# A conditioned decoder block on one core: no spare matmuls between the constants and the first projection

## The chip, the core and the metric

The kernel runs on one NeuronCore of one Trainium2 chip. The metric is the device time of one execution, in microseconds (us); lower is better. Three timed executions of the kernel before are shown, and one execution taken by the hardware profiler.

## What is computed

The reference is one decoder layer over 512 tokens of 1024 features, all in float32. What matters here is how it begins: a vector `c` gives the shifts and scales (`mod`), `x` is normalised and modulated, and the result `h` is multiplied by a wide weight matrix.

```python
c_act = jax.nn.silu(c)
mod = c_act @ w_ada[l] + b_ada[l]                      # (1, 6 * 1024)
shift1, scale1, gate1, shift2, scale2, gate2 = jnp.split(mod, N_MOD, axis=-1)
h = modulate(rmsnorm(x, g_norm1[l]), shift1, scale1)   # (512, 1024)
z = h @ w_in[l]
xr, gr, q, k, v, fl, mg = jnp.split(z, split_idx, axis=-1)
# RG-LRU over xr, forgetting attention over q, k, v, merged by gates,
# then a gated ffn and a last modulated rmsnorm
```

## The kernel before, in words

Each engine has an order of its own, written out by hand, and the engines meet at semaphores. The features lie on the 128 partitions and the 512 tokens along the free dimension. Every float32 matrix is split into a high and a low part of type `fp32r`, and a product is three matmuls (`mm3`, lines 1667 to 1669): low times high, high times low, high times high.

The start is what the change touches, and the orders there are these.

- GpSimd writes the constants: `ident` (the unit matrix), `ones`, `ones_r` and others. TensorE waits for them (`consts`, 8).
- SyncE issues nearly all loads, in this order: `c`, `x` in four blocks, seven small vectors, four blocks of `w_ada` of 1 MB each (`ada_first` 0 to 3), three halves of weight tiles of `w_in`, `ada_first` 4 to 7, and the other halves of these tiles. `ada_first` 6 goes into the buffer of block 0, so it waits until TensorE is done with the first column sum (`ada_mm`, 1).
- ScalarE squares and normalises `x` (lines 612 and 621), copies the transposed blocks out of PSUM (line 626), takes the high parts of the weight tiles (line 637), and when `mod` is there it makes `htmp` and the high part of `h`, feature block by feature block (`h_high`, lines 642 and 645).
- VectorE sums part of the rows of `w_ada` times `c` (lines 1006 and 1009), stores the first scales and shifts (`ada_first_store`, lines 1016, 1019 and 1023), and makes the low parts: `lo_half` for weights (line 1152), `h_low` for `h` (line 1157). Between the two halves of `h` it works on 25 small steps for the recurrence (`lam_first`, `lam_rest`).
- TensorE transposes small vectors (lines 1732, 1759 and 1760), multiplies some rows of `w_ada` with `c` one column at a time (`ada_piece`, line 1711), transposes the four blocks of `x` (`x_transposes`, line 1743), adds what VectorE has summed (`ada_first_total`, line 1719), and then begins the first projection in `project2` (lines 1789 on).

Between these stand calls of `keep_clock(n)`: n float32 matmuls of `ones` with `ident` into PSUM bank 1, which nobody reads. There are four such calls, of 8, 25, 3 and 8 matmuls. The trace has two records for one float32 matmul, so 8 matmuls are 16 records; a transpose is one record.

After the start the projections, the recurrence, the attention, the output projection and the ffn follow, with two weight tiles in a ring. Each load of the ring waits until VectorE is done with the tile before it, so these loads have no time of their own but follow the engines.

Of the kernel before, what the change touches and what calls it, by code (L numbers as in the profile page):

```python
# [81 lines left out]
def hybrid_block(nc, x, c, w_ada, b_ada, g_norm1, w_in, w_rnn_conv, b_rnn_conv, w_lru_a, b_lru_a,  # L82
# [4 lines left out]
    with ctx:  # L87
# [1576 lines left out]
        def _(te):  # L1664
# [38 lines left out]
            def ada_piece(g, v, k, begin=False):  # L1703

                q = 4 * g + 2 * v + k // 4
                te.wait_ge(ada_first_loaded[q], 16)
                if g:
                    te.wait_ge(ada_out, v + 1)
                for j in range(4):
                    at_ = 4 * g + j  # L1710
                    te.matmul(ps[:, 7 - v, at_:at_ + 1], ada_first[:, q % 6, k % 4, P * j:P * j + P], cact[:, k:k + 1],  # L1711
                              start=begin and j == 0, stop=False, skip_group_check=True)

            def ada_first_total(g, v):

                te.wait_ge(ada_part, ada_summed(g, v) + len(ADA_DVE[g, v]))
                for j in range(4):
                    at_ = 4 * g + j
                    ins = te.matmul(ps[:, 7 - v, at_:at_ + 1], (ada_acc, ada_acc2)[v][:, P * j:P * j + P], ones[:, 0:1],  # L1719
                                    start=False, stop=True, skip_group_check=True)  # L1720
                ins.then_inc(ada_mm, 1)

            def keep_clock(n, bank=0):

                for _ in range(n):
                    te.matmul(ps[:, bank, 0:P], ones[:, :], ident[:, :], start=True, stop=True)  # L1726
# [4 lines left out]
            te.wait_ge(vec_a_loaded, 16 * 3)  # L1731
            te.transpose(ps[:, 0, 0:V_ROWS_A], vrows[0:V_ROWS_A, 0], ident[0:V_ROWS_A, 0:V_ROWS_A])\
              .then_inc(vec_mm, 1)
            keep_clock(25, 1)

            def x_transposes(b):
                te.wait_ge(xn1_done, b + 1)
                if b >= 2:
                    te.wait_ge(xT_copied, 2 * b - 2)
                for half in range(2):  # L1740
                    for j in range(4):
                        k = 4 * half + j
                        ins = te.transpose(ps[:, 2 + 2 * (b % 2) + half, P * j:P * j + P],
                                           x_nat[:, b, P * k:P * k + P], ident[:, :])
                    ins.then_inc(xT_mm, 1)
# [2 lines left out]
            x_transposes(0)  # L1748
            x_transposes(1)
            ada_piece(0, 0, 4)  # L1750
            keep_clock(3, 1)
            x_transposes(2)
            ada_piece(0, 1, 0, begin=True)
            x_transposes(3)
# [6 lines left out]
            ada_piece(0, 1, 4)  # L1761
            ada_piece(0, 1, 5)
            ada_first_total(0, 1)
            keep_clock(8, 1)
            te.wait_ge(vec_ok, 2)
            te.wait_ge(xT_copied, 2 * NB)

# [362 lines left out]
```

## Time and profile before

| | us |
|---|---|
| median of three timed executions | 983.5 |
| lowest, highest | 982.2, 983.51 |
| the profiled execution | 983.65 |
| its span, first to last instruction | 981.9 |
| TensorE matmuls busy in it | 968.5 (99%) |
| VectorE, ScalarE busy | 635.5 (65%), 415.8 (42%) |
| mean granted TensorE clock | 0.993 of full |

The page cuts the span into 40 slices of 24.5 us. Each digit is a busy share in tenths, and PEclk is the granted clock in tenths of full speed:

```profile
PE   8999999999999999999999999999999999999997
DVE  3789998522668797853758555777674344754665
ACT  6479777322426354352623373322232222422331
PEclk9899999999999999999999999999999999999999
DMA  9743311334674435432217505666532332233201
```

TensorE is busy nearly all the time. The change lies in the first two slices.

### The profile page before, as it was taken

To read this page: it belongs to the slowest core of one execution; us is meant where nothing else is said; L and a number is where in the kernel's file an instruction comes from. 1 tells how busy PE (TensorE), PEld (TensorE's weight loads), DVE (VectorE), ACT (ScalarE), POOL (GpSimd) and SP (SyncE) were. 2 spreads that over 40 slices of the span, in tenths; PEclk is the share of its full clock that TensorE was granted. 3 is DMA by queue.
4 is the path that set the end of the run, shared out by engine and by line. 5 is a ranking of instruction groups with operands and counts; after the bars stand their busy time and mean duration, and the time that the engine had idled before them with its cause. 6 is when DMAs were issued, how large, how long until landed. Compare 5 with 4: busy or idle time off the path is not lost.

```text
span 981.9 us, 12554 instructions
## 1 busy us (share of the span) xinstructions
PE 968.5 (99%) x4739; PEld 816.5 (83%) x4739; DVE 635.5 (65%) x856; ACT 415.8 (42%) x548; POOL 2.2 (0%) x12
## 2 busy tenths in 40 slices
PE   8999999999999999999999999999999999999997
PEld 8878887788888888989888889888888888888875
DVE  3789998522668797853758555777674344754665
ACT  6479777322426354352623373322232222422331
POOL 0000000000000000000000000000000000000000
PEclk9899999999999999999999999999999999999999
DMA  9743311334674435432217505666532332233201
GB/s 326 249 139 102 102 43 49 96 96 131 210 232 151 153 116 181 129 107 86 86 44 259 192 21 172 196 200 202 180 118 86 105 109 85 86 106 136 100 20 67
DMA packets 105775, 129.37 MB, mean 132 GB/s; under 512 B 4636, under 2 KB 81156, under 8 KB 105612
## 3 DMA queue, kind: packets, MB, share of 16 engines
q1 hardware_dynamic: 105192, 126.75, 39.5%
q10 hardware_dynamic: 548, 2.14, 0.6%
q8 instruction: 23, 0.38, 0.2%
q14 instruction: 12, 0.10, 0.0%
HBM read 126.77 MB, written 2.11 MB: 131 GB/s over the span
## 4 chain that ended last, share of the span: by engine, by line
PE 94%; DVE 3%; DMA 1%; SPq 1%; issue 0%; ACT 0%; DVEq 0%; ACTq 0%
PE ps L1667 30%; PE ps L1669 30%; PE ps L1668 30%; DMA ada_first<-in_w_ada 1%; PE ps L1900 1%; PE ps L1711 1%; DVE wsplit_x L1570 0%; DVE wraw_x L1566 0%; PE ps L1726 0%; PE ps L1719 0%; PE ps L1701 0%; PE ps L1700 0%; PE ps L2017 0%; DVE act_s L1583 0%; SPq L447 0%
## 5 line engine op out<-in xcount | busy, mean ns | idle before, releaser
L1667 PE MATMUL ps<-h,wsplit 128*128 128x512 f32 (+1 forms) x816 | 312.7, 383 | 1.2 <-DVE h L1539 1.2
L1669 PE MATMUL ps<-h,wsplit 128*128 128x512 f32 (+1 forms) x816 | 310.9, 381 | 0.0
L1668 PE MATMUL ps<-h,wsplit 128*128 128x512 f32 (+1 forms) x816 | 310.8, 381 | 0.0
L988 DVE TENSOR_TENSOR wsplit<-wraw,wsplit 128x2048 fp32r<-128x2048 f32 (+2 forms) x79 | 167.0, 2114 | 101.6 <-ACT wsplit L596 64.1
L1667 PEld LDWEIGHTS ps<-h,wsplit 128*128 128x128 f32 x816 | 153.6, 188 | 29.9 <-issue 1.4
L1669 PEld LDWEIGHTS ps<-h,wsplit 128*128 128x128 f32 x816 | 153.4, 188 | 29.5
L1668 PEld LDWEIGHTS ps<-h,wsplit 128*128 128x128 f32 x816 | 153.5, 188 | 28.8
L596 ACT ACTIVATE wsplit<-wraw 128x2048 fp32r<-128x2048 f32 (+2 forms) x69 | 120.9, 1752 | 105.2 <-PE ps L1669 104.8
L1596 DVE SCALAR_TENSOR_TENSOR cv<-ps,vec,cv 128x511 f32<-128x511 f32 (+1 forms) x48 | 35.9, 748 | 55.7 <-ACT cv L945 52.6
L1041 DVE SCALAR_TENSOR_TENSOR ada_acc<-ada_raw,small,ada_acc 128x512 f32<-128x512 f32 x84 | 63.1, 751 | 2.7
L1667 PE MATMUL ps<-wsplit,act_s 128*128 128x512 f32 x160 | 62.3, 390 | 0.7 <-DVE act_s L1583 0.7
L1669 PE MATMUL ps<-wsplit,act_s 128*128 128x512 f32 x160 | 62.3, 389 | 0.0
L1668 PE MATMUL ps<-wsplit,act_s 128*128 128x512 f32 x160 | 62.2, 389 | 0.0
L945 ACT ACTIVATE cv<-ps,vec 128x512 f32<-128x512 f32 x24 | 18.7, 778 | 101.1 <-PE ps L1669 101.1
L1669 PE MATMUL ps<-wsplit,h 128*128 128x256 f32 (+1 forms) x160 | 48.7, 304 | 0.0
L1668 PE MATMUL ps<-wsplit,h 128*128 128x256 f32 (+1 forms) x160 | 48.7, 304 | 0.0
L1667 PE MATMUL ps<-wsplit,h 128*128 128x256 f32 (+1 forms) x160 | 48.7, 304 | 0.0
L929 ACT ACTIVATE wsplit<-wraw 128x2048 fp32r<-128x2048 f32 x10 | 19.2, 1916 | 61.6 <-PE ps L1669 52.4
L1606 DVE TENSOR_TENSOR act<-gg,ps 128x512 f32 (+1 forms) x24 | 16.4, 685 | 34.7 <-PE ps L1669 34.7
L785 ACT ACTIVATE qk<-ps 128x512 fp32r<-128x512 f32 x16 | 9.6, 598 | 63.2 <-PE ps L1669 63.2
L1667 PEld LDWEIGHTS ps<-wsplit,act_s 128*128 128x128 f32 x160 | 30.0, 188 | 7.2 <-issue 1.1
L1669 PEld LDWEIGHTS ps<-wsplit,act_s 128*128 128x128 f32 x160 | 30.0, 188 | 6.3
(248 smaller groups left out, 1415.7 us busy)
## 6 DMA issues: line engine op xcount, KB each, us to landing
wraw<-in_w_ffn_up SPq DMA_DIRECT2D x24, 1024.0 KB, 5.1
wraw<-in_w_in SPq DMA_DIRECT2D x23, 1024.0 KB, 5.3
ada_raw<-in_w_ada SPq DMA_DIRECT2D x16, 1024.0 KB, 6.7
wraw<-in_w_ffn_down SPq DMA_DIRECT2D x10, 1024.0 KB, 4.9
ada_first<-in_w_ada SPq DMA_DIRECT2D x8, 1024.0 KB, 12.1
ada_raw<-in_w_ada_final SPq DMA_DIRECT2D x8, 1024.0 KB, 5.1
wraw<-in_w_in SPq DMA_DIRECT2D x12, 512.0 KB, 3.8
wraw<-in_w_proj_rnn SPq DMA_DIRECT2D x8, 640.0 KB, 4.4
```

Source lines behind the costliest of these rows:

```text
L596: ae.activation(wsplit[:, s, HI, 0:n], wraw[:, s, 0:n], ACT.Copy).then_inc(w_hi, 1)
L929: ae.activation(wsplit[:, s, HI], wraw[:, s], ACT.Copy).then_inc(w_hi, 1)
L945: ae.activation(cv[:, t], ps[:, t, :], ACT.Identity, scale=vec[:, ds(V_FW + 2 * NF + t + 2 * i, 1)], bias=vec[:, ds(V_FB + t + 2 * i, 1)]) ...
L988: ve.tensor_tensor(wsplit[:, s, LO, 0:n], wraw[:, s, 0:n], wsplit[:, s, HI, 0:n].bitcast(F), ALU.subtract).then_inc(w_lo, 1)
L1041: ve.scalar_tensor_tensor(acc[:, :], w, cact[:, k:k + 1], acc[:, :], ALU.mult, ALU.add)\
L1596: ve.scalar_tensor_tensor(cv[:, t, d:T], ps[:, t, 0:T - d], vec[:, ds(V_FW + (2 - d) * NF + t + 2 * i, 1)], cv[:, t, d:T], ALU.mult, ALU.a ...
L1606: ve.tensor_tensor(act[:, 2 * i + t], gg[:, t], ps[:, 2 + t, :], ALU.mult)\
L1667: te.matmul(dst, lhs(LO), rhs(HI), start=start, stop=False)
L1668: te.matmul(dst, lhs(HI), rhs(LO), start=False, stop=False)
L1669: return te.matmul(dst, lhs(HI), rhs(HI), start=False, stop=stop)
L1711: te.matmul(ps[:, 7 - v, at_:at_ + 1], ada_first[:, q % 6, k % 4, P * j:P * j + P], cact[:, k:k + 1], start=begin and j == 0, stop=False, ...
L1900: ins = te.transpose(ps[:, bank, at_:at_ + P], prob[:, t, pcol:pcol + P], ident[:, :])
```

## The change

Three of the four calls of `keep_clock` go: that of 25 matmuls behind the transpose of the first small vectors, that of 3 between the transposes of `x`, and that of 8 ahead of the first projection. The call of 8 right after the constants (line 1730) stays. Nothing else is changed, moved or added.

```diff
             te.transpose(ps[:, 0, 0:V_ROWS_A], vrows[0:V_ROWS_A, 0], ident[0:V_ROWS_A, 0:V_ROWS_A])\
               .then_inc(vec_mm, 1)
-            keep_clock(25, 1)
...
             x_transposes(0)
             x_transposes(1)
             ada_piece(0, 0, 4)
-            keep_clock(3, 1)
             x_transposes(2)
...
             ada_piece(0, 1, 4)
             ada_piece(0, 1, 5)
             ada_first_total(0, 1)
-            keep_clock(8, 1)
             te.wait_ge(vec_ok, 2)
             te.wait_ge(xT_copied, 2 * NB)
```

## Rows read from the trace of the kernel before

**Rows 1.** The page, part 4: who carries the chain that ended last.
```profile
PE 94%; DVE 3%; DMA 1%; SPq 1%; issue 0%; ACT 0%; DVEq 0%; ACTq 0%
```

**Rows 2.** The chain of waits, first 45 us: start us, us, what.
```profile
7.83 14.47 DMA ada_first<-in_w_ada
...
22.34 3.45 PE ps L1711 x16
25.79 1.71 PE ps L1719 x8
27.50 3.62 PE ps L1726 x16
31.12 0.43 PE ps L1667
...
33.32 0.23 PE ps L1667
```

**Rows 3.** Timeline of TensorE: start, us, line, out<-in, xcount [idle before <-releaser].
```profile
3.10 3.78 PE L1726 MATMUL ps<-ident,ones 128*128 128x128 f32 x16 [3.10 <-POOL ones_r L585]
6.68 0.35 PE L1732 MATMUL ps<-ident,vrows 88*128 88x88 f32 x1
6.83 6.75 PE L1726 MATMUL ps<-ident,ones 128*128 128x128 f32 x50
13.42 0.95 PE L1711 MATMUL ps<-small,ada_first 128*128 128x1 f32 x8
14.23 1.95 PE L1743 MATMUL ps<-ident,x_nat 128*128 128x128 f32 x16
...
16.82 0.91 PE L1726 MATMUL ps<-ident,ones 128*128 128x128 f32 x6
...
21.53 0.30 PE L1760 MATMUL ps<-ident,vrows 96*128 96x96 f32 x1
22.34 3.45 PE L1711 MATMUL ps<-small,ada_first 128*128 128x1 f32 x16 [0.51 <-DMA ada_first<-in_w_ada]
...
53.08 0.47 PE L1667 MATMUL ps<-h,wsplit_r 128*128 128x512 f32 x1 [1.05 <-DVE h L1157]
```

**Rows 4.** TensorE by half microseconds: stretch, length, busy (records), clock, DMA share, GB/s.
```profile
8.00:8.50 0.50, 0.50 (x4) 1.00 0.94 359
...
9.00:9.50 0.50, 0.50 (x7) 1.00 0.79 223
...
22.00:22.50 0.50, 0.16 (x2) 1.00 1.10 346
22.50:23.00 0.50, 0.50 (x4) 0.51 1.11 354
...
32.50:33.00 0.50, 0.50 (x3) 0.75 1.06 389
```

**Rows 5.** Timeline of VectorE in the first 62 us.
```profile
13.26 0.48 DVE L1006 TENSOR_SCALAR ada_acc<-ada_first,small 128x512 f32<-128x512 f32 x1 [0.97 <-DMA ada_first<-in_w_ada]
...
29.35 0.69 DVE L1157 TENSOR_TENSOR h<-htmp,h 128x512 fp32r<-128x512 f32 x1 [0.28 <-ACT h L645]
...
48.56 0.17 DVE L1127 TENSOR_SCALAR small<-small 128x10 f32<-128x10 f32 x1
49.25 0.16 DVE L1023 TENSOR_TENSOR mod<-ps,vec 128x4 f32<-128x4 f32 x1 [0.52 <-PE ps L1719]
...
52.24 1.29 DVE L1157 TENSOR_TENSOR h<-htmp,h 128x512 fp32r<-128x512 f32 x2
```

**Rows 6.** Timeline of ScalarE in the first 62 us.
```profile
20.22 1.08 ACT L626 ACTIVATE xT_out<-ps 128x512 f32<-128x512 f32 x2 [0.71 <-PE ps L1743]
...
27.84 0.81 ACT L642 ACTIVATE htmp<-xT_out,mod,small 128x512 f32<-128x512 f32 x1 [1.46 <-DVEq L1027]
```

**Rows 7.** Timeline of SyncE's DMA issues in the first 75 us.
```profile
17.79 8.24 SPq L433 DMA_DIRECT2D ada_first<-in_w_ada  x4
```

**Rows 8.** DMA issues of the same stretch: count, KB each, median us to landing.
```profile
ada_first<-in_w_ada SPq DMA_DIRECT2D x8, 1024.0 KB, 12.1
```

## The prediction

> **What bounds the kernel now.** I read the page's chain first: TensorE carries 94% of it [rows 1], so the kernel is a long row of matmuls, and a microsecond lost by TensorE at the start is lost at the end unless a later wait gives it back. Then the chain of the first 45 us, since the change ends before 31 us: the load of `w_ada` block 3 ends at 22.30, TensorE works from 22.34 to 27.50 on single-column matmuls (24 records), then 3.62 us on the last spare matmuls, and the first projection starts at 31.12 [rows 2]. Third TensorE's own timeline, to see the spare work (16, 50, 6 and 16 records) beside the real work [rows 3], and last the clock by half microseconds. The reader is to see two things there. The clock column says 1.00 at 8 us and at 9 us, but 4 records fit into a half microsecond at the one and 7 at the other [rows 4]: before about 8.9 us the engine ran at its lower level, 1.2 GHz, whatever the column shows before its first change. It then ran at 2.4 GHz until 22.5, fell to 0.50, and rose at 32.75 (0.75 as the mean of 32.5 to 33.0) [rows 4].
>
> What TensorE did before each change: 5.8 us of full-width matmuls without a break (3.10 to 8.9) before the first rise, 5.25 us of the same (27.50 to 32.75) before the second. The fall came in the idle 0.51 us behind single-column matmuls and small transposes, when the last spare matmul was nearly 5 us past [rows 2 to 4].
>
> **The change part by part.** It removes 36 matmuls, 72 records.
>
> The 25: TensorE has nothing to do from about 7.0 us (end of the small transpose) until `ada_first` 0 lands, which is by VectorE's row just before 13.26 [rows 3, 5]. The first `ada_piece` starts at 13.42 now, so the matmuls themselves hold it up by 0.15 us: that is the whole direct gain, -0.15. In their place stand 6.2 us of idling. No row of before has so long an idle time of TensorE after a rise; the nearest is the 0.51 us before 22.34, at whose end the clock was at half. So I take the clock as down at 13.26. (Before, at 13.3, it was up.)
>
> From there the same work at the lower level. Up to the small vectors it is 64 records: three `ada_piece` of 8, 32 transposes, `ada_first_total` of 8. At half clock a record of the single-column kind takes 5.16 us / 24 = 0.215 us [rows 2]; a full-width record takes 3.62 / 16 = 0.226 [rows 2] against 0.91 / 6 = 0.15 with its tail or 1.95 / 16 = 0.12 for the transposes at full clock [rows 3]. The trace has no transpose of `x` at half clock: the bounds are 0.12 (not slower) and 0.233 (3.73 / 16, the spare matmuls of the first call); I take 0.215, since at full clock both kinds go at the same pace, 0.12. 64 x 0.215 = 13.8, and about 0.6 for the two vector transposes (0.30 is the record of one at full clock). So 13.25 + 13.8 + 0.6 = 27.6 instead of 21.83, past the landing at 22.30 that now hides everything earlier. Then the 24 records, 5.2 us, already at half clock today: the total ends at 32.8 instead of 27.50, **+5.3 us**. The 3 matmuls between the transposes, 0.88 us, are in this count by their absence; today they are hidden by the DMA wait at 22.3, so alone they would give nothing.
>
> What else waits for the transposes: ScalarE copies them out, the last ending at 21.30 now and needed by 27.84 [rows 6]; both move alike. SyncE's load of block 6 waits for the first total, which stands ahead of line 1760 (21.5) now and at 27.0 then. Four issues took 8.24 us from 17.79, and a block lands 12.1 us after its issue (median) [rows 7, 8]; block 5, issued about 19.8, is still on its way at 27, so the DMA engines have work and I cost this at 0. If that cover were gone, the price would be the block's delay in issue, up to 5 us, less the 5.3 us by which its reader is late itself: 0.
>
> The 8: when the total is there, VectorE, ScalarE and VectorE need until 30.04 to make the first `h` (line 1157, 29.35 + 0.69) [rows 5], 2.54 us behind 27.50. The projection starts at 31.12, so the last spare matmuls hold it up by **-1.05 us**, gained. In their place TensorE idles 2.6 us and begins the projection cold. Today 1.6 us of it are at half clock (31.12 to 32.75). Then it is as long as a rise takes from the start of dense work, 5.25 us by the nearer of the two cases (5.8 by the other; 1.6 the lower end). A matmul of 512 columns takes 0.43 at half and 0.23 at full clock [rows 2], so each microsecond at half clock wastes 0.47: (5.25 - 1.6) x 0.47 = **+1.7 us** (0 to +2.4).
>
> Downstream: VectorE's line 1023 waits 0.52 us for TensorE at 49.25; its own small steps end at 48.73, and the second half of `h` follows at 52.24, for which TensorE waits 1.05 us at 53.08 [rows 3, 5]. VectorE moves by 5.3, TensorE by 5.3 - 1.05 + 1.7 = 5.95, so TensorE is still the later one and the chain through 49.25 moves by 5.9. From 53 us on, all loads are released by VectorE's steps, nothing is tied to a clock time, and I find no wait that gives it back.
>
> Sum: -0.15 is inside the +5.3; +5.3 - 1.05 + 1.7 = +5.9. The profiled execution took 983.65 (span 981.9 and 1.75 around it), which is 0.15 above the median of the three timed runs. 983.5 + 5.9 = **989.4**, and I say 989.3.
>
> The Trainium skill, "TensorE: Matmul & The Clock Gate", Part 4 (PE-mode transpose), says that the full clock does not engage for transposes, as they do not count as a busy engine in the same way. By it the 32 transposes could not lift the clock and the sum above stands; the rows show neither, since all 32 ran at 1.00 here. The same page's Part 1 (The HAM clock gate) tells of a half-rate default that sustained activity releases, with no word on its kind. By that the clock could come up among the transposes, which is the first rival. No row decides between the two.
>
> **The rivals.** (1) The clock comes up among the transposes and holds: **not slower**. TensorE works without a break from 13.25; a rise 5.8 us later, as at the start, is at 19.1. By then 27 records are done; the other 37 take 37 x 0.115 = 4.3, the vectors 0.5, so 23.9; if the clock then held for 2 us more and fell, about 17 of the 24 records go at 0.115 and 7 at 0.215: 27.4, -0.1 against now. Then -1.05 and, with the projection from 30.0 cold until 32.75 or a little later, +0.5 to +0.9: -0.6 to 0, 983.2. For it: the dense row of 16 transposes. Against it: both rises seen came after nothing but full-width matmuls, and the fall at 22.5 came where there were only transposes and single columns. It decides at whether TensorE is at full clock for the vectors' transposes. Chance 0.10.
>
> (2) It comes up late in the transposes and falls again at once, as it does at 22.5 now: 57 records by 22.5, 7 x 0.215 + 0.6 + 5.2 more, 29.8, +2.3; then -1.05 and +1.7: +2.9, 986.4. Chance 0.14.
>
> (3) The change does not do what it says: the clock is the same with and without the spare matmuls. Then only the -1.05 counts, of which VectorE lets through 0.5 at 49.25: 983.0. Against it: the pace of 4 and 7 records. Chance 0.08.
>
> (4) The forecast and a late load of block 6 or of what is behind it in the queue: +1 to +3 more, 991.5. Chance 0.06.
>
> **How the numbers follow.** The forecast has 0.62, with its own range from +3.9 (no longer cold projection, transposes a little quicker) to +6.6: 987.4 to 990.2. I let the range of 8 in 10 reach down over rival (2), 985.0, and up to 990.5; rivals (1) and (3) and most of (4) lie outside. What a measurement can tell here is 0.2%, 2 us. Slower: the forecast, (2) and (4), less a little for a smaller (2): 0.78. Same: (1), (3) and that little: 0.19. Faster has no case with a price of 2 us: 0.03.
>
> **What would show it.** In the profile after, the first record of line 1711 starts near 13.3 and two `ada_piece` and two blocks of transposes go at 4 to 5 records per microsecond, not 9; line 1760 ends near 27.6, and the wait for `ada_first` before the next line-1711 group is gone; line 1719's first total pair ends near 32.8; TensorE idles 2.6 us, released by VectorE's line 1157; the first line 1667 starts near 35.4, and the clock is 0.50 for about 5 us of it. TensorE's restart at 53.08 is near 59. Wrong would be 7 records per half microsecond anywhere before the first projection, or a chain where a load stands between 27 and 45 us.

## The result, and the profile after

The kernel after the change takes 989.53 us in the median of 20 timed executions, against 982.33 for the kernel before (20 executions as well). The ratio is 1.0049, with a 95% interval of 1.0032 to 1.0065: slower, by half a per cent. (The ratio is near that of the means, 987.34 to 982.56. The medians stand at 1.0073, since the median of the changed kernel lies in the upper of its two groups.)

The median hides what matters: the 20 times of the changed kernel fall into two groups with nothing between them, 8 from 982.6 to 984.02 and 12 from 988.77 to 991.26. Those of the kernel before lie from 981.06 to 984.46 in one group. I call the two the quicker and the slower kind of execution; neither is a disturbed run. Both kinds have been profiled, the slower in the first profile, the quicker in a third one (`e9_changed_third`, below).

The page of the slower kind, with the span and the first slices of TensorE and its clock:

```profile
span 988.0 us, 12410 instructions
PE   6899999999999999999999999999999999999997
PEclk7699999999999999999999999999999999999999
```

Its chain of waits (start us, us, what) answers to [rows 2]:

```profile
13.26 1.83 PE ps L1711 x8
15.10 3.52 PE ps L1742 x16
...
27.34 3.26 PE ps L1711 x16
30.60 1.72 PE ps L1719 x8
32.34 0.17 DVE mod L1023
...
34.16 0.70 DVE h L1157
35.00 0.77 PE ps L1667
35.76 0.43 PE ps L1668
```

(Line 1742 is line 1743 of before, since the first of the removed lines stands ahead of it.) The block load that ended at 22.30 has left the chain: TensorE itself is the bound from 13.26 to 32.3. TensorE's timeline shows the idle time that the 25 used to fill, and the one ahead of the projection:

```profile
13.26 1.83 PE L1711 MATMUL ps<-small,ada_first 128*128 128x1 f32 x8 [6.37 <-DMA ada_first<-in_w_ada]
14.96 3.65 PE L1742 MATMUL ps<-ident,x_nat 128*128 128x128 f32 x16
...
35.00 0.77 PE L1667 MATMUL ps<-h,wsplit_r 128*128 128x512 f32 x1 [2.69 <-DVE h L1157]
...
59.11 0.47 PE L1667 MATMUL ps<-h,wsplit_r 128*128 128x512 f32 x1 [1.05 <-DVE h L1157]
```

Sixteen transposes take 3.65 us where they took 1.95 [rows 3]. The half microseconds (columns as in [rows 4]) show where the clock fell, at 10.0 us and so 3.1 us into the idle time that the 25 used to fill, and that it was low from the first real work to beyond 40 us:

```profile
10.00:10.50 0.50, 0.00 (x0) 0.53 1.02 319
...
15.00:15.50 0.50, 0.50 (x4) 0.50 1.05 385
...
40.50:41.00 0.50, 0.50 (x3) 0.75 0.99 203
41.00:41.50 0.50, 0.50 (x4) 1.00 0.46 105
```

The number behind x counts every record that touches the stretch. So x4 and x7 do not mean that 4 or 7 records fit into it, as the prediction puts it: at 0.22 and 0.12 us each, 2.3 and 4.2 do. The ratio of nearly two is what tells the two levels of the clock apart.

And the quicker kind of the same kernel, TensorE's timeline and its half microseconds: the clock comes up at 19.8, before the third block of transposes, which takes 1.07 us for 8 instead of 1.95, and falls again at 26.6, at the end of the last column sum:

```profile
15.49 3.65 PE L1742 MATMUL ps<-ident,x_nat 128*128 128x128 f32 x16
18.93 1.35 PE L1711 MATMUL ps<-small,ada_first 128*128 128x1 f32 x8
20.15 1.07 PE L1742 MATMUL ps<-ident,x_nat 128*128 128x128 f32 x8
...
25.72 1.05 PE L1719 MATMUL ps<-ones,ada_acc 128*128 128x1 f32 x8
29.45 0.77 PE L1667 MATMUL ps<-h,wsplit_r 128*128 128x512 f32 x1 [2.69 <-DVE h L1157]
```

```profile
19.00:19.50 0.50, 0.50 (x5) 0.50 1.03 381
19.50:20.00 0.50, 0.50 (x5) 0.73 1.05 381
...
20.50:21.00 0.50, 0.50 (x7) 1.00 1.05 354
...
26.50:27.00 0.50, 0.27 (x3) 0.60 0.97 373
...
33.00:33.50 0.50, 0.50 (x3) 0.58 1.05 385
```

Ahead of this rise TensorE had done nothing since 6.7 us but single-column matmuls and transposes, from 13.79 on.

### The profile page after: what moved, and what is told of

Same layout as the page of the kernel before. It is cut to its first block, busy times and chain, and to the rows that moved or that the text cites. A ratio compares the mean times of both kernels' runs of the same rounds, so it can differ in the third digit from the quotient of the medians.

```text
span 988.0 us, 12410 instructions
## 1 busy us (share of the span) xinstructions
PE 966.1 (98%) x4667; PEld 813.5 (82%) x4667; DVE 635.8 (64%) x856; ACT 416.0 (42%) x548; POOL 2.2 (0%) x12
## 4 chain that ended last, share of the span: by engine, by line
PE 95%; DVE 3%; DMA 1%; issue 0%; SPq 0%; ACT 0%; DVEq 0%; ACTq 0%
PE ps L1667 30%; PE ps L1669 30%; PE ps L1668 30%; PE ps L1711 1%; PE ps L1897 1%; DMA ada_first<-in_w_ada 1%; PE ps L1742 1%; PE ps L1719 0%; DVE wsplit_x L1570 0%; DVE wraw_x L1566 0%; PE ps L1701 0%; PE ps L1700 0%; PE ps L2014 0%; DVE act_s L1583 0%; DVE act_x L1574 0%
## 5 line engine op out<-in xcount | busy, mean ns | idle before, releaser
L1667 PEld LDWEIGHTS ps<-h,wsplit 128*128 128x128 f32 x816 | 153.6, 188 | 30.1 <-issue 1.4
```

The costliest lines, as they stand in the source:

```text
L1667: te.matmul(dst, lhs(LO), rhs(HI), start=start, stop=False)
```

## The experiments

The theory at this point: the 25 kept the clock up through the wait for `w_ada`; without them the transposes start at half clock, and whether they lift it differs from execution to execution. Rivals: the last 8 carry the loss (a projection that starts cold), and transposes do not count for the clock, so that the quicker kind has another cause.

### e1_only_25_gone, e2_only_last_8_gone, e11_only_3_gone: one part at a time

```diff
# e1
-            keep_clock(25, 1)
# e2
-            keep_clock(8, 1)        # the one ahead of the projection
# e11
-            keep_clock(3, 1)
```

> Only the 25 spare matmuls are taken out; the 3 and the last 8 stay. Theory (the 25 carry the loss): in the executions in which the clock stays at half, the first total pair ends near 32.3 us as after the full change; the last 8 then run 32.3 to 35.9 and the projection starts near 36.0 instead of 35.0, with only about 2 to 4 us of it at half clock: 988 to 990 us. In the executions in which the clock comes up among the transposes, 982 to 984. Both kinds should be seen. Rival (the loss comes from the last 8, the projection starting cold): 982 to 984 in all executions.

> Only the last 8 spare matmuls are taken out; the 25 and the 3 stay. Theory: the projection starts 1.0 us earlier, near 30.1, and its stretch at half clock grows from 1.6 us to 3 to 5 us, so the restart at 53 us moves by -0.4 to +0.6 us and the time by the same: within 0.1% of the kernel before, in one mode. Rival (the last 8 decide when the clock rises): at half clock to beyond 36 us, +2 us or more.

> Only the 3 spare matmuls between the transposes are taken out. By the prediction's step they give nothing (0 within 0.1%). By what the run with only the 25 kept showed (0.16% slower, where the last 8 alone are worth 0.07%) they hold the clock up in part of the executions: +0.5 to +1.5 us in the median.

Without the 25: 986.89 (983.87 to 989.24, 6 executions), ratio 1.0045, interval 1.0027 to 1.0063, the same as the whole change. Both ends of the expected spread are there, but with times between them (986.5, 987.3, 987.6), which I had not expected. That with the 3 and the 8 still there the clock can come up at more places is a guess; no execution of the middle times was profiled. Without the last 8: 983.04, ratio 1.0007 (0.9997 to 1.0017), one group. Without the 3: 983.30, ratio 1.0001 (0.9989 to 1.0013). The prediction's two terms for the last 8, -1.05 and +1.7, come to +0.65 us, and 1.0007 is +0.7. So the 25 carry the loss, and the other two show no effect by themselves that is clear of the intervals.

In the profile without the last 8 the projection starts at 29.24 instead of 30.77 (near 30.1 had been expected), behind 2.69 us of idling, and stays at half clock until 33.1, 3.8 us long, as expected; TensorE's timeline:

```profile
24.71 1.84 PE L1719 MATMUL ps<-ones,ada_acc 128*128 128x1 f32 x8
29.24 0.77 PE L1667 MATMUL ps<-h,wsplit_r 128*128 128x512 f32 x1 [2.69 <-DVE h L1157]
```

### e3_only_25_kept and e4_25_as_transposes: does a transpose count?

```diff
# both: the 3 and the last 8 are gone; e4 has in place of keep_clock(25, 1):
+            for _ in range(50):
+                te.transpose(ps[:, 1, 0:P], ident[:, :], ident[:, :])
```

> The kernel after the change with the 25 spare matmuls put back (the 3 and the last 8 are gone). Theory: all of the loss goes, 982 to 984 us in every execution, the clock at full level for the transposes of x and falling near 20 to 22.5. Rival (the 3 hold the clock between the transposes): the clock falls one step earlier, near 19 us, so 13 to 30 more records at half clock, +1.5 to +3 us in part of the executions.

> As the run before, but the 25 spare matmuls are 50 spare transposes of the unit matrix (50 records of 128 columns either way) into the same bank. Theory (transposes count for the clock like any full-width matmul): the same pace of 7 records per half microsecond from about 9 us, and the same time, 982 to 984 us. Rival (transposes do not count): the clock stays at or falls to half before 13 us, the x transposes run at 4 to 5 records per half microsecond, 987 to 990 us in all executions.

984.09, ratio 1.0016 (1.0005 to 1.0028), and 984.80, ratio 1.0015 (1.0002 to 1.0028). The two are alike, and no execution of either is above 986.6, where the changed kernel has most of its own at 988.8 and more. But both expectations, 982 to 984 in every execution, were missed: 6 of 11 and 7 of 12 lie above 984, up to 985.8 and 986.5. Part of the loss stays, in part of the executions, which is what the rival for the 3 said. The trace with the 50 transposes, TensorE's timeline and its half microseconds:

```profile
6.83 6.62 PE L1735 MATMUL ps<-ident 128*128 128x128 f32 x50
```

```profile
8.00:8.50 0.50, 0.50 (x4) 1.00 0.95 376
...
9.00:9.50 0.50, 0.50 (x7) 1.00 0.75 248
...
19.00:19.50 0.50, 0.50 (x5) 0.61 1.02 375
```

From 4 records in a half microsecond to 7 at about 9 us, the same place as with the matmuls of before [rows 4] (the column's 1.00 at 8 us is, as there, no reading). Alone this rise is weak evidence, since 3.6 us of full-width matmuls stood ahead of the 50. But nothing except transposes kept TensorE busy from 9 to 13.3 us at the full level, and the rise at 19.8 in the quicker kind of the changed kernel came behind nothing but single columns and transposes. Transposes count. This contradicts the rule of the Trainium skill ("TensorE: Matmul & The Clock Gate", Part 4, PE-mode transpose) as the prediction drew on it: by it the clock would not have come up or stayed up in either case. The measurement decides.

Both runs are a little slower than the kernel before (about 1.5 us by the ratios). In the trace of the second the clock falls at 19.1, between transposes and single columns, 3.4 us earlier than in [rows 4], and the 24 single-column records take about 5 us again. The absence of the 3 can do this: without them TensorE waits 0.64 to 0.78 us for ScalarE ahead of the third block of transposes in the traces of e3, e4 and e11. In that of e11 the clock falls at 20.0; in that of e3 it holds until 24.5. The times of e11 don't show a loss (1.0001), so how much of the 1.5 us this is stays open.

### e6_all_four_gone and e7_12_instead_of_25: no spare matmul at all, and half of the 25

```diff
# e6: the changed kernel, and besides
-            keep_clock(8, 1)        # the one behind the constants
# e7: the kernel before with
-            keep_clock(25, 1)
+            keep_clock(12, 1)
```

> The first call of 8 is taken out as well, so no spare matmul is left. Theory: by 13.3 us the clock is down with or without it, so nothing changes against the kernel after the change: the same two kinds of executions, 983 to 984 and 989 to 990, and the same median within 0.3%. Rival (the first 8 matter for the later rise): all executions 989 to 990.

> 12 spare matmuls instead of 25 (the 3 and the last 8 stay), so TensorE works to about 10.5 us and then idles 2.7 us. Theory (the clock falls in long idle times and the loss is that fall): in part of the executions the clock is still up at 13.3 (982 to 984), in the others it falls just before or behind it (986 to 989): a median between that of the kernel before and that of only the 25 gone, 983.5 to 986.5. Rival (a rise holds over any idle time under 5 us): 982 to 984 in all.

With none left: 986.59 in the median, six executions from 982.37 to 983.76 and six from 989.42 to 990.19, ratio 1.0032 (1.0011 to 1.0053). The same two kinds as after the change; the first 8 show no effect without what follows them. The median here is a number at which no execution lies. With 12: 986.13, ratio 1.0021 (1.0008 to 1.0034), 7 of 11 executions from 985.9 to 986.8 and 4 from 982.7 to 984.6. Its trace:

```profile
6.66 2.88 PE L1726 MATMUL ps<-ident,ones 128*128 128x128 f32 x24
13.43 1.83 PE L1711 MATMUL ps<-small,ada_first 128*128 128x1 f32 x8 [3.90 <-DMA ada_first<-in_w_ada]
```

```profile
12.00:12.50 0.50, 0.00 (x0) 1.00 1.02 389
...
13.00:13.50 0.50, 0.07 (x1) 0.79 1.00 385
...
14.00:14.50 0.50, 0.50 (x4) 0.50 1.07 397
```

The 24 records take 0.12 us each, so the clock was at its full level when they ended at 9.5. It falls at 13.3, 3.8 us into the idle time and just ahead of the first real work at 13.43. It comes up between the last two blocks of transposes, at 23.5, and falls at 26.9, ahead of most of the 24 single-column records: much the course of the prediction's second rival. In e11 the spare matmuls end 0.95 us ahead of the load, and the clock holds. So spare matmuls that end well ahead of the load lose their worth, at least in part of the executions. No run has few spare matmuls placed right ahead of the load, so the idle time and the number of matmuls are not told apart.

### e5_changed_again, e9_changed_third, e10_transposes_together: what makes the two kinds

```diff
# e5, e9: the changed kernel as it is. e10: the changed kernel with
             x_transposes(0)
             x_transposes(1)
-            ada_piece(0, 0, 4)
             x_transposes(2)
+            ada_piece(0, 0, 4)
```

> The kernel after the change once more, for a trace of an execution of its quicker kind. Theory (in about half of the executions the clock comes up among the transposes of x): with a chance of a half a time of 983 to 984 us, clock up between 16 and 20 us, the first total pair ending 25 to 28 us and the projection starting 28 to 30.5. Else the same as the first trace: 989 to 990, at half clock until about 5.5 us behind the start of the projection.

> The kernel after the change, as the control of the next run on the same chip and for a trace of the quicker kind. Theory: two kinds of executions, 983 to 984 and 989 to 991, with nothing between, each in a third to two thirds of them.

> The kernel after the change with one call moved: ada_piece(0, 0, 4) stands behind x_transposes(2) instead of ahead of it, so that 24 transposes (5.2 us at half clock) follow one another instead of 16 (3.5 us). No work is added or taken out. Theory (transposes count, and whether the clock comes up depends on how long they go on unbroken, against something that differs from execution to execution): the slower kind becomes rare or goes, median 982.5 to 985. Rival (transposes do not count, and the quicker kind has another cause): two kinds in the same shares as in the control, 983.5 and 989.7.

The first gave the slower kind again (991.29, clock low to 40.65). The control gave 5 executions from 982.52 to 983.29 and 7 from 989.60 to 990.26, ratio 1.0044 (1.0022 to 1.0066), and the trace of the quicker kind shown above. With the transposes together, at the same work: 986.79, from 983.03 to 988.28, ratio 1.0026 (1.0013 to 1.0040). The group at 990 is gone: none of 12, against 7 of 12 in the control on the same chip. In its place stand 7 from 986.5 to 988.3; the other 5 lie from 983.0 to 985.2. So the order of the same work decides whether the slowest kind exists, as the theory said, and my expected median (982.5 to 985) was missed. That it is the unbroken length of the transposes that counts is not shown apart from the later place of the single columns. The profile is of that new group, and its half microseconds show why:

```profile
20.50:21.00 0.50, 0.50 (x5) 0.59 1.09 352
...
22.50:23.00 0.50, 0.50 (x7) 1.00 1.10 346
...
24.00:24.50 0.50, 0.50 (x5) 0.82 1.08 352
24.50:25.00 0.50, 0.50 (x5) 0.50 1.07 373
```

The clock came up at 20.9, after the 24 transposes, and fell at 24.3, ahead of the 24 single-column records, which then went at half clock. That is the prediction's second rival (up late, down at once, 986.4).

### e8_four_more_at_22us and e12_seven_more: a version that beats both?

```diff
# both: the kernel before, with
             ada_first_total(0, 0)
+            keep_clock(4, 1)
# e12 besides
             ada_piece(0, 1, 4)
+            keep_clock(3, 1)
             ada_piece(0, 1, 5)
```

> The kernel before with 4 more spare matmuls behind the first column sum, where TensorE waits 0.51 us for block 3 of w_ada. Theory (the fall at 22.5 us comes from sparse work): the clock stays up longer, the 24 records behind it take 2.8 instead of 5.2 us at the price of 0.4 us, but the projection cannot start before 28.7 us since ScalarE's weight halves end at 26.4: 1 to 2.5 us quicker than before, 980 to 981.5. Rival (the 24 single-column records pull the clock down anyway within a microsecond): 0.4 us slower than before.

> The kernel before with 4 more spare matmuls behind the first column sum, as in the run that beat it, and 3 more between the two ada_piece calls behind block 3. Theory: the 3 cost 0.66 us at full clock but hide behind ScalarE's weight halves (26.4 us), and keep the clock up to the projection in more executions: 0 to 1 us quicker than with 4 more, 980.5 to 982. Rival: they come too late and cost 0.7 to 1.3 us where the clock is already down, 982 to 983.5.

With four more: 981.87 against 983.08 for the kernel before on the same chip, ratio 0.9991 with an interval of 0.9983 to 1.0000, so at the edge of what can be told (980 to 981.5 had been expected); the highest of 12 executions is 982.98, where those of before reach 985.25 there, and one 988.22. (So the kernel before is not wholly free of slow starts either.) The trace:

```profile
22.43 1.87 PE L1711 MATMUL ps<-small,ada_first 128*128 128x1 f32 x16
24.16 1.19 PE L1719 MATMUL ps<-ones,ada_acc 128*128 128x1 f32 x8
25.21 3.50 PE L1726 MATMUL ps<-ident,ones 128*128 128x128 f32 x16
28.47 0.48 PE L1667 MATMUL ps<-h,wsplit_r 128*128 128x512 f32 x1
```

The 24 records take 2.9 us instead of 5.2 [rows 2], and the projection starts 2.3 us earlier (28.47 instead of 30.77 in the same view) and at full clock. Between them the clock was down, from 24.9 to 28.3: it fell although TensorE had been busy in every half microsecond since 3.5 us, and most of the last 16 spare records ran at half clock (3.50 us). That much is seen in this one execution, whose span is 979.2. With seven: 982.32, ratio 1.0002 (0.9982 to 1.0022), ten executions from 981.34 to 983.21 and two at 989.2 and 989.5, of which there is no trace. In its profile the records keep the pace of the full level from 8.5 us on throughout, and it is no quicker (span 980.9). `ada_first` 0 landed late in it (TensorE waits 1.02 us for it and begins at 14.29, 1.2 us later than in e8), which can explain a part of the 1.7 us between the two spans. More spare work is not better.

## Why the prediction was right, and where it was not

It forecast 989.3; the median is 989.53. The sum describes the slower kind of execution, and from trace to trace it stands term by term:

- The fall of the clock in the idle time: the prediction took it as down by 13.26 with no row to show it; it fell at 10.0.
- The transposes and single columns at half clock: predicted 64 records in 13.8 us, vectors 0.6, 24 records in 5.2, together +5.3 on the store at line 1023. Measured: 13.46 (13.26 to 26.72), 0.62 and 4.98, and line 1023 at 32.34 instead of 27.53, **+4.8**. The price of a record was 0.210, not 0.215, and the unseen one, a transpose at half clock, was within its bounds: 16 in 3.5 us, 0.22.
- The last 8: predicted -1.05. From line 1023 to the projection it is 2.66 us now and was 3.59: **-0.9**. In their place TensorE idles 2.69 us, as forecast (2.6).
- The longer cold stretch: predicted rise 5.25 us after the start, +1.7. It came at 40.75, 5.75 after 35.00: (5.75 - 1.6) x 0.47 = **+1.95**. Not in the sum was the first matmul, 0.77 us on the chain instead of 0.43. The 5.25 was one value of many: in the seven traces in which TensorE idles and then begins the projection at half clock with a reading of the column, the rise comes 3.8 (e2) to 6.1 us (e3) after the start, worth +1.0 to +2.1.
- Downstream: the restart of TensorE at 59.11 instead of 53.08, **+6.0** (predicted 5.9), and the span 988.0 instead of 981.9, +6.1. Nothing gives it back. VectorE's timeline has the store at 55.28, and it is TensorE that is late there:

```profile
55.28 0.16 DVE L1023 TENSOR_TENSOR mod<-ps,vec 128x4 f32<-128x4 f32 x1 [1.20 <-PE ps L1719]
```

- Block 6 of `w_ada`: its issue waited (four issues in 10.26 us instead of 8.24 [rows 7]) and no engine waited for it. Cost 0, as predicted.

```profile
17.41 10.26 SPq L433 DMA_DIRECT2D ada_first<-in_w_ada  x4
```

What was wrong is the weight of the first rival, the clock that comes up among the transposes. It had 0.10; 13 of the 33 executions of the changed kernel (8 of 20, 0 of 1, 5 of 12) have the times of that kind; one of them was profiled. Its price was right: 983.2 predicted, 982.5 to 984.0 measured, and the rise at 19.8 where 19.1 was worked out. Its trace also has what the prediction named as a sign of being wrong, x7 ahead of the first projection. The step that failed is the argument against it, that both rises seen had come after full-width matmuls only: in that trace single columns and transposes alone came ahead of the rise. The second rival (0.14) is not seen in the changed kernel at all, but is what e7 and e10 run into.

The time was hit closer than it deserved, by luck in two places. The first is the share of the two kinds: with 6 of 12 in either, as in e6, the median is 986.6. The second is the base. The 983.5 was the median of three executions; twenty of the same kernel have 982.33, and on that the sum gives 988.2. The slower kind has its median at 989.8, so it is 7.5 us above the kernel before and not 5.9. The trace of before (983.65) was one of its own slower executions, which is why the traces differ by 6.1 only.

What differs between two executions of one program is not shown by any run; that it acts through the moment at which the clock changes is. In the idle time the clock fell at 10.0 and 9.9 in the two traces of the slower kind and at 9.5 in that of the quicker, which is a hint and no more.

My point on the 3 (alone they give nothing) holds for the times of e11.

## What to carry to other kernels

A spare matmul is worth what it does for the real ones behind it: price the work that would run at half clock (here 64 + 24 records at 0.1 us each, and 0.47 us for each microsecond of a cold projection), against the time that the spare ones add, which is nearly zero under a load's wait (0.15 us here). How near they have to reach to the load is seen at two places: ended 0.95 us ahead of it, they held the clock (e11); with 12 of the 25, ended 3.9 us ahead, about half of the loss was back (0.21% of e1's 0.45%, though the intervals overlap). And before believing a median, look at the single times: two groups mean that something is decided anew in each execution, and a change can move the shares rather than the times.

## What the hardware showed that was not expected

- Transposes count for TensorE's clock. In the quicker kind it came up at 19.8 us behind single columns and transposes only, and in e4 50 spare transposes gave the same course as the spare matmuls (from x4 to x7 at about 9 us in both).
- The clock can fall while TensorE is busy without a gap, where the work is single columns: at 24.9 us in e8.
- The same program has two times 6 to 7 us apart, by whether the clock comes up behind 16 unbroken transposes (3.65 us at half clock); with 24 unbroken the slowest group is gone (e10).
- The clock column of the profile reads 1.00 before its first change whatever the clock is. Where spare matmuls are gone altogether (e6) this goes on to 41 us, and the mean clock of such an execution reads 0.999 though it is the slower kind:

```profile
14.00:14.50 0.50, 0.50 (x4) 1.00 1.06 397
```
